# Two-layer encoder: in the first layer one token tile takes all output weights before the other, and the first split of the dense layer moves into the norm stage

## What is computed

```
for layer in range(2):
    hn = rmsnorm(h, mix_norm_pre[layer])
    proj = hn @ w_in[layer]                       # u, q, k, v
    y_pool = pool_mixer(u, ...)                   # 512 channels
    y_na = neighbourhood_attention(q, k, v, ...)  # 512 channels
    mix = concat([y_pool, y_na]) @ w_out[layer]   # the output projection, 1024 x 1024
    h = h + rmsnorm(mix, mix_norm_post[layer])
    hn = rmsnorm(h, ffn_norm_pre[layer])
    f = swiglu(hn) if layer == 0 else moe_swiglu(hn)   # dense, then 2 of 8 experts
    h = h + rmsnorm(f, ffn_norm_post[layer])
```

## Time and profile before

| | |
|---|---|
| median of three runs | 1310.09 us (1308.52 to 1312.76) |
| the profiled execution | 1313.94 us, span 1312.1 us |
| TensorE busy in it | 1287.3 us, 98% of the span |
| mean granted TensorE clock | 0.992 |
| VectorE, ScalarE, GpSimd busy | 404.4, 286.7, 107.7 us |
| first layer's output projection and its norms | about 83 to 116 us of the span |
| mixture of experts | about 480 us to the end |

### The profile page before, as it was taken

How to read it: one execution, slowest core, us unless ns; L and a number is a source line. 1 busy time by engine, 2 the same in 40 slices (tenths; PEclk the granted TensorE clock), 3 DMA queues, 4 the chain that set the end, 5 groups by cost and what they waited for, 6 DMA issues and landing times.

```text
span 1312.1 us, 31069 instructions
## 1 busy us (share of the span) xinstructions
PE 1287.3 (98%) x14401; PEld 795.7 (61%) x14401; DVE 404.4 (31%) x565; ACT 286.7 (22%) x433; POOL 107.7 (8%) x240
## 2 busy tenths in 40 slices
PE   8999999999999999999999999999999999999996
PEld 8888999999989863354353364345353355336443
DVE  6777545555576750030110130030030031031011
ACT  4665444444465630000000000000000000000101
POOL 4133400000000307300000000000000000000000
PEclk9899999999999989999999999999999999999999
DMA  9537855555544399999999999999999999999994
GB/s 306 216 134 223 266 192 193 194 193 193 189 146 175 125 425 427 427 421 394 429 424 425 425 425 426 426 425 425 425 424 425 427 425 424 425 426 425 426 424 178
DMA packets 66868, 443.50 MB, mean 338 GB/s; under 512 B 4504, under 2 KB 10656, under 8 KB 42160
## 3 DMA queue, kind: packets, MB, share of 16 engines
q1 hardware_dynamic: 64592, 433.58, 81.3%
q0 software_dynamic: 2144, 7.90, 2.1%
HBM read 439.36 MB, written 2.10 MB: 336 GB/s over the span
## 4 chain that ended last, share of the span: by engine, by line
PE 91%; DMA 4%; DVE 2%; SPq 1%; ACT 1%; issue 0%; ACTq 0%; DVEq 0%
PE psum L1072 38%; PE psum L1081 18%; PE psum L726 9%; PE psum L728 9%; PE psum L727 9%; DMA unit<-in_moe_w_down 3%; PE psum L1016 2%; PE psum L1027 1%; PE psum L823 1%; PE psum L814 1%; DMA ring<-in_w_in 1%; SPq L384 1%; PE psum L840 1%; ACT pt L1225 1%; PE psum L755 1%; DVE hs L1520 0%
## 5 line engine op out<-in xcount | busy, mean ns | idle before, releaser
L1072 PE MATMUL psum<-unit,xT 128*32 128x448 f32 x5376 | 507.0, 539 | 0.1
L1072 PEld LDWEIGHTS psum<-unit,xT 128*32 128x32 f32 x5376 | 174.3, 110 | 327.5 <-issue 325.4
L1081 PE MATMUL psum<-unit,hid 128*32 128x256 f32 x4704 | 259.1, 379 | 3.2 <-DMA unit<-in_moe_w_down 3.2
L1081 PEld LDWEIGHTS psum<-unit,hid 128*32 128x32 f32 x4704 | 151.4, 110 | 108.4 <-issue 5.3
L1739 DVE TENSOR_TENSOR hidp<-hid,psum 128x448 f32<-128x448 f32 x42 | 38.5, 917 | 535.4 <-PE psum L1072 535.4
L726 PE MATMUL psum<-hT_hi,w_hi 128*128 128x256 f32 x656 | 184.0, 280 | 0.9 <-DVE w_lo L1419 0.8
L1419 DVE TENSOR_TENSOR w_lo<-ring,w_hi 128x2048 fp32r<-128x2048 f32 x64 | 148.0, 2321 | 116.6 <-ACT w_hi L1184 116.3
L728 PE MATMUL psum<-hT_hi,w_lo 128*128 128x256 f32 x656 | 182.7, 279 | 0.0
L727 PE MATMUL psum<-hT_lo,w_hi 128*128 128x256 f32 x656 | 182.7, 278 | 0.0
L1184 ACT ACTIVATE w_hi<-ring 128x2048 fp32r<-128x2048 f32 x71 | 135.3, 1911 | 65.1 <-PE psum L728 52.8
L726 PEld LDWEIGHTS psum<-hT_hi,w_hi 128*128 128x128 f32 x656 | 124.2, 189 | 3.1 <-issue 2.5
(11 more groups left out here) (253 smaller groups left out, 944.8 us busy)
## 6 DMA issues: line engine op xcount, KB each, us to landing
unit<-in_moe_w_gate SPq DMA_DIRECT2D x64, 1792.0 KB, 32.6
unit<-in_moe_w_up SPq DMA_DIRECT2D x64, 1792.0 KB, 27.2
unit<-in_moe_w_down SPq DMA_DIRECT2D x64, 1792.0 KB, 32.0
ring<-in_dense_w_gate SPq DMA_DIRECT2D x8, 2048.0 KB, 9.0
ring<-in_dense_w_up SPq DMA_DIRECT2D x8, 2048.0 KB, 9.0
ring<-in_dense_w_down SPq DMA_DIRECT2D x8, 2048.0 KB, 8.3
ring<-in_w_in SPq DMA_DIRECT2D x6, 2048.0 KB, 8.7
ring<-in_w_out SPq DMA_DIRECT2D x4, 2048.0 KB, 7.7
```

Of the source, the lines that this page charges most:

```text
L1072: ins = mm(bank(half, s)[quad(j)], xT[:, s, dt, :], w[:, at:at + FJ], start=dt == 0, stop=dt == DT - 1)
L1081: ins = mm(down_out[s][quad(j)], e[:, half, s, t, :], w, start=half == t == 0 and s != 2, stop=half == 1 and t == FT - 1, skip_group_check ...
```

## The change

Three edits, in layer 0 alone; layer 1 computes in the order it had.

1. `project` takes half 1 for tile 0 only. Tile 1's four products with half 1 go into `project_last`, where tile 1 now takes the halves 1, 2 and 3 on its first 512 columns and then on the others. `half_done` for half 1 comes with the latter.
2. ScalarE makes the high part of half 12 no longer at the end of the mixing stage but in the first `norm_pair`, between the squares of tile 1's first and second bank.
3. VectorE makes the low part of half 12 at the end of the first `norm_pair`, behind the last copy of the transposed tokens.

```diff
--- before.py
+++ after.py
@@ -860,17 +860,19 @@
                 def project(half, src):
 
                     for et in range(2):
-                        for t in range(NT):
+                        for t in range(1 if layer == 0 else NT):
                             ins = project_part(half, et, t, src)
-                    ins.then_inc(half_done, 1)
-
-                def project_last(src):
+                    if layer:
+                        ins.then_inc(half_done, 1)
+
+                def project_last(src, attention):
 
                     def step(half, et, t, j):
                         w = [a.rearrange("p (t n) -> p t n", t=2)[:, et, j * C4:(j + 1) * C4]
                              for a in split_half(h0 + 8 + half)]
                         e = 2 * (half % 2) + et
-                        return product((pa, pb)[t][:, j * C4:(j + 1) * C4], [a[:, e, t * P:(t + 1) * P] for a in src], w,
+                        still = [a[:, e, t * P:(t + 1) * P] for a in (attention if half == 1 else src)]
+                        return product((pa, pb)[t][:, j * C4:(j + 1) * C4], still, w,
                                        False, (half, et) == (3, 1))
 
                     for half in (2, 3):
@@ -880,10 +882,10 @@
                             if half == 3:
                                 ins.then_inc(bank_done, 1)
                     for j in range(2):
-                        for half in (2, 3):
+                        for half in (2, 3) if layer else (1, 2, 3):
                             for et in range(2):
                                 ins = step(half, et, 1, j)
-                            if (j, half) != (0, 2):
+                            if j or half == 3:
                                 ins.then_inc(half_done if j else bank_done, 1)
 
                 if layer == 0:
@@ -923,7 +925,7 @@
                 pe.wait_ge(yaT_ready, 3 * (layer + 1))
                 project(1, (yaT_hi, yaT_lo))
                 pe.wait_ge(ypT_ready, layer + 1)
-                project_last((ypT_hi, ypT_lo))
+                project_last((ypT_hi, ypT_lo), (yaT_hi, yaT_lo))
 
             def dense():
                 h0 = 2 * MIX_LOADS
@@ -1243,6 +1245,8 @@
                         else:
                             act.wait_ge(bank_done, 3 * n + 2 * t + j + 1)
                         square(pt23[:, t, j * C4:(j + 1) * C4], (pa, pb)[t][:, j * C4:(j + 1) * C4], post + 16 * (1 - j))
+                        if (n, t, j) == (0, 1, 0):
+                            split_to(2 * MIX_LOADS + 1)
                     act.wait_ge(sum_ready, 4 * n + 2 * t + 1)
                     root_of_sums(post).then_inc(rms_post, 1)
                     if t:
@@ -1331,7 +1335,7 @@
                     c = 4 * layer + g
                     ins = act.activation(ypT_hi[:, g, :], pc[:, g * S:(g + 1) * S], ACT.Copy, scale=cols[:, c:c + 1])
                 ins.then_inc(ypT_hi_ready, 1)
-                split_to(h0 + 13 if layer == 0 else h0 + 12)
+                split_to(h0 + 12)
 
             def dense():
                 h0 = 2 * MIX_LOADS
@@ -1522,6 +1526,8 @@
                             (hs_half, hs_ready)[j], 1)
                 for t, k in ((0, 1), (1, 0), (1, 1)) if n < 2 else ((1, 1),):
                     tokens_lo(n + 1, t, k)
+                if n == 0:
+                    split_to(2 * MIX_LOADS + 1)
 
             def last_norm(value):
                 dve.wait_ge(gpost_back, 16)
```

## The result

The kernel got slower, by more than forecast. Five runs have a median of 1317.44 us (1314.61 to 1317.70), beside 1310.58 for the kernel before in five (1308.52 to 1312.76). The ratio is 1.0044, 95% interval [1.0032, 1.0057], so +5.8 us [4.2, 7.5], where +0.85 was forecast. The profiled execution has a span of 1315.9 us, against 1312.1.

What follows compares the result with a forecast made beforehand. TensorE was taken to bound the kernel, 91% of the chain that ended last. Stall +1.05, tile 1's norms -0.20 and splits 0 gave +0.85 us on a median of 1310.09, so 1310.9 us, range 1308.2 to 1313.6.

Steps and rivals of the forecast that it cites:

- Edit 1, the cost: Projection, before the first matmul on half 2: TensorE stalls for `ypT_lo`, 1.05 us, within bounds of 0.76 to 1.11.
- the free restart: Same wait: the weight load is pulled ahead of the waiting matmul, so the stall is only 0.76 us.
- the row's: Same wait: the weight load waits too; restart 0.15 and longer first step 0.20 make the upper bound, 1.11 us.
- Edit 1, the gain: Tile 1's norms after the projection: `h` follows TensorE's end by 1.84 us instead of 2.05; -0.20 us.
- Edit 2: ScalarE's high part of half 12, before tile 1's second squares: 0.8 us of cover, cost nothing.
- Edit 3: VectorE's low part of half 12, behind the token copies: 0.9 us of slack to its first reader, cost 0 to 0.1.
- half 12 is late: Either moved split overruns its cover of 0.8 or 0.2 us: about 1 us more, 1311.9 us; chance 0.06.
- The clock rival: TensorE's new 1.05 us gap at 93.3 us lowers its granted clock: 3.4 us more, 1314.3 us; chance 0.07.
- The sum: Stall +1.05, tile 1's norms -0.20, both splits 0: +0.85 us at the dense layer's start and at the end.

Runs made afterwards that it cites:

- experiment 4: experiment 1's kernel, with two of tile 1's four products with half 1 kept ahead of the wait for `ypT_lo`; ratio 1.0011.
- Experiment 5: The changed kernel with the old order of products and no wait for half 12's low part before the dense layer's first half; ratio 1.0027.
- experiments 3 and 8: The changed kernel with seven, then four, useless matmuls ahead of the wait for half 12's low part; ratios 1.0018 and 1.0039.
- experiment 1: The changed kernel, with TensorE starting the dense layer's first half without the wait for its low part; median 1315.53 us, ratio 1.0021.
- experiments 1 and 10: The same kernel timed twice: the changed kernel without the wait for the low part before the dense layer's first half; ratios 1.0021 and 1.0022.
- experiment 2: The kernel before, with only VectorE's low part of half 12 moved to the end of the first norm stage; ratio 1.0043.

## Why the prediction was wrong

- **Edit 1, the cost: right.** `ypT_lo` ended at 90.80 + 1.66 = 92.46, TensorE was at the wait at 91.47 + 0.23 = 91.70: 0.76 us, as worked out. The restart cost 0.05 us to the first matmul and 0.11 in the first step (92.51 to 92.85 against 0.23), not 0.15 and 0.20. The 0.20 had been read at 90.34, where TensorE hadn't waited but passed from the pooling matmuls to the projection. The projection's end moved by 0.93, forecast 1.05. The truth lies between the free restart that the rule of the Trainium skill would give (TensorE: Matmul & The Clock Gate, Step-by-step: what each phase is for), 0.76, and the row's, 1.11. The trace doesn't bear out that rule for a load whose matmul waits: it started with its matmul, at 92.51.
- **Edit 1, the gain: right.** Tile 1's `h` came 108.21 - 106.36 = 1.85 us behind TensorE's end, forecast 1.84; -0.20 as forecast, and -0.21 alone in experiment 4.
- **Edit 2: right for this kernel.** ScalarE's half 12 ran 103.87 to 105.79, the squares behind it waited for TensorE and began at 106.56, so 0.77 us of cover, forecast 0.8 (timeline of ScalarE after, below). Experiment 5 shows that this cover is a product of edit 1: without it the same split costs 0.75 us.

```profile
103.87 1.92 ACT L1186 ACTIVATE w_hi<-ring 128x2048 fp32r<-128x2048 f32 x1 [0.74 <-PE psum L728]
...
106.56 0.60 ACT L1227 ACTIVATE pt<-psum 128x512 f32<-128x512 f32 x1 [0.77 <-PE psum L728]
```

- **Edit 3: the step that failed.** The prediction said that the first reader of half 12's low part "is the matmul group at 118.56 plus shift", with 0.9 us of slack. That is the first that reads it, but not the first that waits for it. `split_half` waits for `split_ready` 13 in the dense loop ahead of `open_half`, at line 965, and the description of the kernel above has that wait only further down, inside `open_half`. In the kernel before, the low part was ready at 98.24 + 2.29 = 100.53 us, 14 us ahead, so no row showed a wait there (timeline of VectorE before):

```profile
98.24 2.29 DVE L1419 TENSOR_TENSOR w_lo<-ring,w_hi 128x2048 fp32r<-128x2048 f32 x1 [1.75 <-ACT w_hi L1184]
```

  Worked out with it, from the same rows, the price would have been 117.63 - 114.72 = 2.9 us. Measured: 2.88 in the changed kernel, 2.86 alone, 0 with the wait gone. The rival "half 12 is late" named the right half, but by another way, a split that overruns its cover, and at about 1 us; the split itself was on time (forecast 117.63 plus shift, that is 117.63 - 1.59 + 0.73 = 116.8; it ended at 116.68).
- **The clock rival: a fall did come, in another place.** It was put at the 1 us gap at 93 us, where the clock stayed at 1.00. The gap that brought it down was the 3.61 us at 113 us, which followed from the failed step. It cost 2.2 us (5.79 - 3.61), not 3.4; experiments 3 and 8 took 2.3 away. The comparison that the rival was weighed by, a gap "less than half of 2.31", is weaker than it looked, since gaps of 2.03 to 2.31 us went both ways.
- **The sum.** 0.93 - 0.20 + 2.88 + 2.18 = 5.79, which is the measured shift of half 13. Of the profiled execution's +3.8: -1.59 ahead of the mark, +5.79, -1.27 from half 13 to the second layer's pooling (1.1 of it because halves 13 to 17 ran at 113.3 ns instead of 117.8), and +0.87 from there to the end, a stretch that took 855.7 to 858.1 us in the twelve traces whatever the kernel. Without the step that failed, the sum of +0.85 would have been close: experiment 1's kernel has +0.70 at the first dense matmul and, with an opening at the quicker pace, +0.54 at half 13. Its own ratio, 1.0021, is lifted by the runs at the slow pace, as far as their times tell: 12 of 24 runs at 1315 us or over in experiments 1 and 10, beside 6 of 58 for the kernel before.

## What to carry to other kernels

When a producer is moved later, look for the first instruction that waits for its semaphore, in every helper that stands ahead of the reader, and not for the first that reads the data; a wait that is satisfied long before leaves no row. Price a gap on TensorE together with the work behind it at the lower clock: 2.9 us of waiting became 5.1. And where a kernel's runs fall into two groups, compare stage times between marks in the trace before the medians.

## What the runs showed of the hardware

- Matmuls of 128x256 in the fast float32 format, each with its own weight load, ran at 113.3 or 117.8 ns from start to start at the same granted clock, for stretches of 20 us and more, in executions of one kernel. Over 1488 of them this made 6.7 us between two traces of it (experiments 1 and 10). No run of 23 with one full float32 matmul ahead of half 13 was in the upper group of times, 15 of 36 without it were; the halves directly behind it ran at the slow pace all the same.
- TensorE's clock stayed up over gaps of 1.85 to 1.89, 2.23 and 2.31 us and fell behind gaps of 2.03 to 2.31 and 3.61 us, so at 2.2 to 2.3 us both were seen at one and the same place in the kernel. The same gap of 3.61 cost 1.4 us in one kernel (experiment 2) and 2.2 in another (after).
- A matmul behind a wait began 0.05 us after VectorE's end, its weight load no earlier than itself, and the step behind it was 0.11 us longer than the usual 0.23 (after, at 92.51).
